# Moving the router's turn and product behind the last chunks of the output projection in an encoder layer

## The chip, the cores and the metric

The kernel runs on one core of a Trainium2 chip. The time is that of the device in microseconds (us), the median over the runs shown. The engines are TensorE (PE, its weight loads apart as PEld), VectorE (DVE), ScalarE (ACT), GpSimd (POOL), and SyncE (SP), which issues nearly all transfers.

## The reference

One layer of an encoder: a token mixer (attention over latents beside a short convolution), cross attention to 256 memory tokens, and a mixture of 32 experts, each followed by a residual and a layer norm. The tokens are 1024 of a prompt and 8 groups of 16 samples, each with memory keys and values of its own. The part that matters here is the second step, and the router's logits behind it:

```python
def cross_attend(x, mk, mv, w_xq, w_xo):
    q = (x @ w_xq).reshape(B, S, X_HEADS, X_HEAD_DIM)
    sc = jnp.einsum('bqhd,bmhd->bhqm', q, mk).astype(jnp.float32) * X_SCALE
    p = jax.nn.softmax(sc, axis=-1).astype(mv.dtype)
    o = jnp.einsum('bhqm,bmhd->bqhd', p, mv).reshape(B, S, D_MODEL)
    return o @ w_xo
...
x = layer_norm(ALPHA * x + a, lp['ln1_g'], lp['ln1_b'])
x = layer_norm(ALPHA * x + cross_attend(x, mk, mv, lp['w_xq'], lp['w_xo']), lp['ln2_g'], lp['ln2_b'])
x = layer_norm(ALPHA * x + hier_moe(x, lp), lp['ln3_g'], lp['ln3_b'])
...
logits_g = (xt @ lp['w_router_group']).astype(jnp.float32) + lp['b_router_group'].astype(jnp.float32)
logits_e = (xt @ lp['w_router_expert']).astype(jnp.float32).reshape(T, N_GROUPS, EXPERTS_PER_GROUP)
```

D_MODEL is 1024, the four memory heads are 256 wide, and the router has 4 + 32 = 36 columns.

## The kernel before

Every engine has its own program, written out by hand, and they meet in counting semaphores. The tokens are nine tiles of 128 rows: tiles 0 to 7 the prompt, tile 8 the samples. The change lies in one stage: the output projection of the cross attention (w_xo), tile by tile, and woven into it the cross attention of the eight sample groups, one group to one prompt tile.

**TensorE.** `outward(t, ks)` multiplies tile t by chunks ks of w_xo, eight chunks in all, in three products of high and low halves (`three_products`, L911, six matmuls of 512 columns to a chunk). It writes the PSUM tile M[t % 2]. Between the pairs of chunks stand the steps of sample group t and of what is left of group t-1:

- `weigh_memory_rows(t-1)` (L1063) weighs the values, `turn_memory_rows(t-1)` turns the result (two transposes).
- `turn_memory(t, 0)` and `turn_memory(t, 1)` turn the keys of group t (eight transposes each, to T[0]); ScalarE copies the first half out (L1494), VectorE the second (L1913).
- `memory_scores(t)` (L1048) computes the scores, sixteen matmul records over four strips of 32 columns. `turn_weights(t)` turns the softmax weights (two transposes).
- `turn_x2(t-1)` turns the normed rows of tile t-1 (eight transposes to T[0]), ScalarE copies them to x2T (L1483), and `route_rows(t-1)` (L1101) multiplies them by the router: eight matmuls, sixteen records, of 36 columns into M[(t-1) % 2].

All transposes are recorded at L689. Since tile t+1 uses the same PSUM tile as the logits of t-1, `outward` opens with

```python
                        else:
                            pe.wait_ge(logits_done, 2 + t - 1)
```

**VectorE**, for each tile: the sample's query rows (L1911), the second half of the turned keys (L1913), the scores' maximum (L1915), the reciprocal of the sum (L1917); `add_logits(t-1)` (L1851), which adds the router's bias and frees the PSUM tile; then, when projection t is done (product_ps), `add_rows` (L1754 to L1760: residual sum, statistics) and `norm_rows` (L1764, L1767). Between these two, GpSimd works out the inverse deviation (L2118, L2120). GpSimd also splits the rows of a later tile (`out_low`, L2173), of the last tile too.

**ScalarE**, for each tile: the high half of the rows of tile t+1 (L1467), the weighed rows of group t-1 (L1472), the first half of the turned keys (L1494), the turned rows of group t-1 (L1476), `turn_x2(t-1)`, that is the copy to x2T (L1483), exp of the scores (L1499), the turned weights (L1502).

**SyncE**, for each tile: values of group t (L604), keys of group t+1 (L601), the store of normed tile t-1 (L598), and the load of the residual rows of tile t+1 (L594), which waits for turn_x2(t-1), because it overwrites what that step reads. The first half of expert 0's weights (L625) is queued behind the last of these.

Behind the eight prompt tiles TensorE runs weigh_memory_rows(7), turn_x2(7), turn_memory_rows(7), route_rows(7) and the whole of projection 8; then come the router's ranks (L1132 to L1153) and the expert stage.

Of the kernel before, what the change touches and what calls it, by code (L numbers as in the profile page):

```python
# [49 lines left out]
def encoder_layer_kernel(nc, A, O):  # L50
# [4 lines left out]
    P, D, NT, PT = 128, 1024, 9, 8  # L55
# [54 lines left out]
    with ctx:  # L110
# [572 lines left out]
        def _(pe):  # L683
# [3 lines left out]
            def transposes(out, rows, n, width=P):  # L687
                for k in range(n):
                    got = nc.tensor.transpose(out[:, k * P:(k + 1) * P] if width == P else out[0:width, k * P:(k + 1) * P],  # L689
                                              rows[:, k * width:(k + 1) * width], ident)  # L690
                return got
# [214 lines left out]
            def three_products(out, hi, lo, k):  # L906

                for x, parts in ((hi, (high, low)), (lo, (high,))):
                    for c in (0, 512):
                        for part in parts:  # L910
                            got = nc.tensor.matmul(out[:, c:c + 512], x[k], part(k)[:, c:c + 512],  # L911
                                                   start=(k == 0 and x is hi and part is high), stop=(k == KT - 1 and x is lo))
                return got

            def chunks(rows):
                return [rows[:, k * P:(k + 1) * P] for k in range(KT)]
# [125 lines left out]
            def memory_scores(b):  # L1042
                pe.wait_ge(mkT_lo, b + 1)
                pe.wait_ge(mkT_hi, b + 1)
                pe.wait_ge(sxq_ready, b + 1)
                for h in range(XH):
                    for c in (0, 1):
                        got = nc.tensor.matmul(T[1][h * 32:(h + 1) * 32, 0:MEM], qx_b[:, 2 * h + c, :], mkT_b[:, 2 * h + c, :],  # L1048
                                               start=(c == 0), stop=(c == 1))
                got.then_inc(sb_ps, 1)  # L1050

            def turn_weights(b):
                pe.wait_ge(sb_exp, NB + b + 1)
                transposes(T[1][:, 256:512], px_b, 2).then_inc(pTb_ps, 1)
# [18 lines left out]
            def outward(t, ks):  # L1073
                u = t % 2
                for k in ks:
                    if k == 0:
                        pe.wait_ge(rows_high, 2 * NT + t + 1)
                        pe.wait_ge(o_low, t + 1)
                        if t < 2:
                            pe.wait_ge((oT_first, oT_second)[u], 4)  # L1080
                        else:
                            pe.wait_ge(logits_done, 2 + t - 1)
                    if t == 0:
                        pe.wait_ge(w_low, 3 * KT + k + 1)
                    got = three_products(M[u], chunks(rows_hi[u]), chunks(rows_lo[u]), k)
                    if t == PT:
                        got.then_inc(w_used, 1)
                if k == KT - 1 and t < PT:
                    got.then_inc(product_ps, 1)
# [15 lines left out]
            for t in range(PT):  # L1105
                outward(t, (0, 1))
                if t > 0:
                    weigh_memory_rows(t - 1)
                if t > 1:
                    pe.wait_ge(x2T_ready, t - 1)  # L1110
                turn_memory(t, 0)
                outward(t, (2, 3))
                if t > 0:
                    turn_memory_rows(t - 1)
                turn_memory(t, 1)
                outward(t, (4, 5))
                if t > 0:
                    turn_x2(t - 1)
                memory_scores(t)
                if t > 0:  # L1120
                    route_rows(t - 1)
                outward(t, (6, 7))
                turn_weights(t)
            weigh_memory_rows(NB - 1)
            turn_x2(PT - 1)
            turn_memory_rows(NB - 1)
# [131 lines left out]
        def _(act):  # L1258
# [220 lines left out]
            def turn_x2(t):  # L1479
                act.wait_ge(rowsT_ps, 2 * NT + t + 1)  # L1480
                if t > 0:
                    act.wait_ge(router_ps, t)
                nc.scalar.copy(x2T.rearrange("p k c -> p (k c)"), T[0][:, :]).then_inc(x2T_ready, 1)  # L1483

            out_high(0)
            for t in range(PT):
                if t < PT - 1:
                    out_high(t + 1)
                if t > 0:
                    memory_rows(t - 1)  # L1490
                act.wait_ge(mkT_ps, 2 * t + 1)
                if t > 0:
                    act.wait_ge(sb_ps, NB + t)
                nc.scalar.copy(mkT_b[:, :, 0:P], T[0][:, :].rearrange("p (k c) -> p k c", k=KT)).then_inc(mkT_lo, 1)  # L1494
                if t > 0:
                    memory_rows_turned(t - 1)
                    turn_x2(t - 1)
                act.wait_ge(sb_negmax, NB + t + 1)
                nc.scalar.activation(px_b, T[1][:, 0:MEM], ACT.Exp, bias=negmax[0][:, 0:1], scale=1.0,  # L1499
                                     accum_out=rsum[0][:, 0:1]).then_inc(sb_exp, 1)  # L1500
                act.wait_ge(pTb_ps, NB + t + 1)
                nc.scalar.copy(pxT_b.rearrange("p c q -> p (c q)"), T[1][:, 256:512]).then_inc(pTb_ready, 1)  # L1502
            memory_rows(NB - 1)
# [115 lines left out]
        def _(dve):  # L1619
# [133 lines left out]
            def add_rows(n, u, x, r):  # L1753
                nc.vector.scalar_tensor_tensor(r[u], x[u], ALPHA, M[u][:, :], ALU.mult, ALU.add).then_inc(sum_done, 1)  # L1754
                dve.wait_ge(sum_done, n + 1)
                nc.vector.bn_stats(stats[u][:, 0:6], r[u][:, 0:512])
                nc.vector.bn_stats(stats[u][:, 6:12], r[u][:, 512:]).then_inc(dve_step, step.next())
                dve.wait_ge(dve_step, step.value())
                dve.sem_inc(waited, 1)
                nc.vector.bn_aggr(moments[u][:, :], stats[u][:, :]).then_inc(var_ready, 1)  # L1760

            def norm_rows(n, u, x, r, gain, shift):
                dve.wait_ge(var_ready, n + 1)
                nc.vector.scalar_tensor_tensor(r[u], r[u], moments[u][:, 0:1], gain, ALU.subtract, ALU.mult).then_inc(dve_step, step.next())  # L1764
                dve.wait_ge(dve_step, step.value())
                dve.wait_ge(rstd_ready, n + 1)
                return nc.vector.scalar_tensor_tensor(x[u], r[u], rstd[u][:, 0:1], shift, ALU.mult, ALU.add)  # L1767
# [81 lines left out]
            def add_logits(t):  # L1849
                dve.wait_ge(router_ps, t + 1)  # L1850
                nc.vector.tensor_tensor(logits[:, t, :], M[t % 2][:, 0:NG + NE], b_router[:, :], ALU.add).then_inc(logits_done, 1)  # L1851
# [53 lines left out]
            for t in range(NT):  # L1905
                u = t % 2
                if t < PT:
                    b = t
                    if b > 0:
                        dve.wait_ge(sb_ps, NB + b)  # L1910
                    nc.vector.tensor_copy(qx_b[:, :, 0:ROWS], qxT_s[:, :, b * ROWS:(b + 1) * ROWS]).then_inc(sxq_ready, 1)  # L1911
                    dve.wait_ge(mkT_ps, 2 * b + 2)
                    nc.vector.tensor_copy(mkT_b[:, :, P:], T[0][:, :].rearrange("p (k c) -> p k c", k=KT)).then_inc(mkT_hi, 1)  # L1913
                    dve.wait_ge(sb_ps, NB + b + 1)
                    nc.vector.tensor_reduce(negmax[0][:, 0:1], T[1][:, 0:MEM], AX.X, ALU.max, negate=True).then_inc(sb_negmax, 1)  # L1915
                    dve.wait_ge(sb_exp, NB + b + 1)
                    nc.vector.reciprocal(rinv[b % 2][:, 0:1], rsum[0][:, 0:1]).then_inc(sb_p, 1)  # L1917
                    if t > 0:
                        add_logits(t - 1)
                    dve.wait_ge(product_ps, PT + t + 1)  # L1920
                else:
                    add_logits(PT - 1)
                    pick_experts(slice(0, PT), PT)
                    split_gate_up(0, range(5))
                    dve.wait_ge(w_used, 3 * KT)
                dve.wait_ge(x_in[u], 16 * (3 * (5 - u) + t // 2))
                add_rows(NT + t, u, xr2, res2)
                norm_rows(NT + t, u, xr2, res2, gain2, shift2).then_inc(norm_ready, 1)
            slots = slot_id.rearrange("p t k -> p k t")

# [345 lines left out]
```

## Time and profile before

| | |
|---|---|
| median of 3 runs | 1724.16 us (1723.03 to 1727.54) |
| the profiled execution | 1727.54 us, its span 1725.5 us |
| TensorE busy | 1606.8 us, 93% of the span |
| TensorE's weight loads | 1291.3 us, 75% |
| VectorE busy | 993.1 us, 58% |
| ScalarE busy | 752.6 us, 44% |
| GpSimd busy | 256.9 us, 15% |
| mean granted clock | 0.976 |

The span is the time from the first to the last instruction of the profiled execution. Busy shares are means over stages that differ. The chain that ended last is followed back from the last instruction: at each step to what released it. Its pieces are cut where the next begins, while the timeline gives each instruction's full duration; so the same matmuls appear a little longer there. The granted clock is TensorE's: 1.00 is 2.4 GHz, 0.50 is 1.2 GHz.

### The profile page before, as it was taken

The page shows a single profiled execution, that of the slowest core. Times are in us where ns is not written, and L with a number is a line of the kernel's source. Part 1 is how long each engine was busy: PE and PEld are TensorE (multiplying, and loading weights), DVE is VectorE, ACT ScalarE, POOL GpSimd, SP SyncE. Part 2 cuts the span into 40 slices and gives each one's busy share as a digit, 9 for nine tenths or more (in the row PEclk, how much of TensorE's full clock was granted, in tenths as well). Part 3 has the DMA queues.
Part 4 walks back from the last instruction along what each step waited for, and adds up shares of the span by engine and source line. Part 5 has one row for each costly group of instructions (what it writes and reads, how often), then busy time and mean ns, then how long its engine had stood idle before and what let it go on. Part 6 is the DMA issues. An engine that isn't in the chain of part 4 may idle for free.

```text
span 1725.5 us, 21728 instructions
## 1 busy us (share of the span) xinstructions
PE 1606.8 (93%) x8282; PEld 1291.3 (75%) x8282; DVE 993.1 (58%) x1347; ACT 752.6 (44%) x1062; POOL 256.9 (15%) x210
## 2 busy tenths in 40 slices
PE   8999999799998899999999989899999999999966
PEld 4578877467766688899877867788888888888842
DVE  1410111366765365422255447888889898898936
ACT  2311111322334301322242213678878777888834
POOL 0000000000006174000011121121111111111104
PEclk9999999999999999999999996999999999999988
DMA  9510111600002354400045554799999999999967
GB/s 353 214 63 33 65 53 47 241 20 17 13 12 98 131 170 176 171 25 13 1 162 180 172 171 171 284 383 385 372 385 378 380 389 383 395 380 376 362 237 295
DMA packets 134295, 351.77 MB, mean 204 GB/s; under 512 B 24498, under 2 KB 27186, under 8 KB 128708
## 3 DMA queue, kind: packets, MB, share of 16 engines
q1 hardware_dynamic: 124084, 330.69, 52.0%
q0 software_dynamic: 9216, 18.89, 2.9%
q10 hardware_dynamic: 912, 1.05, 0.3%
q8 instruction: 56, 0.92, 0.2%
q14 instruction: 27, 0.22, 0.0%
HBM read 322.19 MB, written 43.15 MB: 212 GB/s over the span
## 4 chain that ended last, share of the span: by engine, by line
PE 61%; DMA 18%; DVE 13%; ACT 4%; issue 3%; SPq 1%; POOL 0%; DVEq 0%; POOLq 0%; ACTq 0%
DMA beside<-in_w_exp_up 16%; PE M L911 12%; DVE rounded L1628 10%; PE T L753 6%; PE M L744 5%; PE M L1159 5%; PE T L689 4%; PE M L816 3%; PE T L806 3%; PE M L689 2%; PE T L970 2%; PE T L972 2%; PE T L971 2%; ACT rounded L1516 2%; PE M L999 2%
## 5 line engine op out<-in xcount | busy, mean ns | idle before, releaser
L1159 PE MATMUL M<-rounded 128*128 128x512 f32 x2304 | 547.9, 395 | 11.1 <-DVE conv_w_rows L1959 5.6
L1628 DVE TENSOR_TENSOR rounded<-beside,rounded 128x1024 fp32r<-128x1024 f32 (+2 forms) x394 | 467.8, 1234 | 113.8 <-ACT rounded L1516 56.6
L1159 PEld LDWEIGHTS M<-rounded 128*128 128x128 f32 x2304 | 429.4, 189 | 104.3 <-issue 13.7
L1516 ACT CAST rounded<-beside 128x1024 fp32r<-128x1024 f32 x256 | 259.2, 1049 | 95.5 <-DMA beside<-in_w_exp_up 88.4
L911 PE MATMUL M<-rounded 128*128 128x512 f32 x864 | 209.6, 397 | 3.0 <-ACT rounded L1388 1.6
L911 PEld LDWEIGHTS M<-rounded 128*128 128x128 f32 x864 | 160.4, 190 | 36.2 <-issue 2.2
L1526 ACT CAST rounded<-beside 128x1024 fp32r<-128x1024 f32 x128 | 125.3, 1048 | 18.3 <-DMA beside<-in_w_exp_down 15.9
L2200 POOL DMA_INDIRECT expert_rows<-beside,route_out x32 | 45.1, 1410 | 375.0 <-ACT beside L1557 355.1
L689 PE MATMUL T<-tables,arena 128*128 128x128 f32 x572 | 80.4, 287 | 19.0 <-DMA arena<-in_mem_prompt 7.1
L1341 ACT ACTIVATE arena<-T,negmax 128x384 f32<-128x384 f32 (+3 forms) x64 | 47.4, 741 | 114.5 <-DVE negmax L1705 114.5
L689 PEld LDWEIGHTS T<-tables,arena 128*128 128x128 f32 x572 | 70.2, 148 | 36.3 <-issue 12.7
L1628 DVE TENSOR_TENSOR rounded<-T,rounded 128x512 fp32r<-128x512 f32 (+1 forms) x82 | 81.7, 1000 | 26.7 <-ACT rounded L1401 18.2
L806 PE MATMUL T<-arena 96*128 96x384 f32 (+3 forms) x192 | 71.8, 489 | 10.8 <-issue 10.8
L816 PEld LDWEIGHTS M<-arena 128*128 128x128 f32 x576 | 71.8, 191 | 10.3 <-issue 7.7
L744 PE MATMUL M<-rounded,x_high 128*128 128x416 f32 (+1 forms) x270 | 70.4, 374 | 6.6 <-DVE x_low L1628 6.6
L970 PE MATMUL T<-rounded 128*128 128x256 f32 x256 | 73.1, 285 | 2.4 <-issue 2.4
L816 PE MATMUL M<-arena 128*128 x576 | 72.5, 271 | 0.7
L971 PE MATMUL T<-rounded 128*128 128x256 f32 x256 | 72.4, 283 | 0.0
L972 PE MATMUL T<-rounded 128*128 128x256 f32 x256 | 72.4, 283 | 0.0
L2193 POOL DMA_INDIRECT beside<-x_rows,route_tok x32 | 50.4, 1575 | 142.0 <-PE T L1200 121.0
L753 PE MATMUL T<-rounded,x_high 128*128 128x512 f32 x270 | 65.3, 394 | 0.0
L753 PEld LDWEIGHTS T<-rounded,x_high 128*128 128x128 f32 x270 | 50.7, 188 | 11.7
(302 smaller groups left out, 2121.3 us busy)
## 6 DMA issues: line engine op xcount, KB each, us to landing
beside<-in_w_exp_gate SPq DMA_DIRECT2D x64, 1024.0 KB, 7.9
beside<-in_w_exp_up SPq DMA_DIRECT2D x64, 1024.0 KB, 11.1
beside<-in_w_exp_down SPq DMA_DIRECT2D x32, 2048.0 KB, 11.4
arena<-x_rows SPq DMA_DIRECT2D x27, 512.0 KB, 4.6
x_rows<-arena SPq DMA_DIRECT2D x18, 512.0 KB, 3.2
arena<-expert_rows SPq DMA_DIRECT2D x9, 1024.0 KB, 12.9
arena<-in_x_prompt SPq DMA_DIRECT2D x16, 512.0 KB, 4.1
arena<-in_cache_mem_k SPq DMA_DIRECT2D x8, 1024.0 KB, 5.7
```

Source lines behind the costliest of these rows:

```text
L689: got = nc.tensor.transpose(out[:, k * P:(k + 1) * P] if width == P else out[0:width, k * P:(k + 1) * P], rows[:, k * width:(k + 1) * widt ...
L744: got = nc.tensor.matmul(M[u][:, at:at + c1 - c0], x[:, k * P:(k + 1) * P], part[k][:, c0:c1], start=(k == 0 and part is w_in_high and x i ...
L753: got = nc.tensor.matmul(T[u][:, c:c + CW], x[:, k * P:(k + 1) * P], part[k][:, GC + c:GC + c + CW], start=(k == 0 and part is w_in_high a ...
L806: got = nc.tensor.matmul(T[n % 2][:, c:c1], qT[u][0:HW, i * P:(i + 1) * P], kT[u][0:HW, c:c1], start=True, stop=True)
L816: got = nc.tensor.matmul(o, prT[n % 2][:, c, :], value[:, c, ds(h * DV, DV)], start=(c == 0), stop=(c == i))
L911: got = nc.tensor.matmul(out[:, c:c + 512], x[k], part(k)[:, c:c + 512], start=(k == 0 and x is hi and part is high), stop=(k == KT - 1 an ...
L970: nc.tensor.matmul(out, high(k)[:, d * P:(d + 1) * P], x1T[:, 0, k], start=(k == 0), stop=False)
L971: nc.tensor.matmul(out, high(k)[:, d * P:(d + 1) * P], x1T[:, 1, k], start=False, stop=False)
L1159: got = nc.tensor.matmul(out, x[xs], (high, low)[ws](w)[:, c:c + 512], start=(first and n == 0), stop=(last and n == 2))
L1516: nc.scalar.copy(high(c), w_raw[c // 4][:, c % 4, :]).then_inc(gu_high, 1)
L1526: nc.scalar.copy(high(8 + c), w_raw[2][:, c, :]).then_inc(down_high, 1)
L1628: return nc.vector.tensor_tensor(out, x, highs.bitcast(f32), ALU.subtract)
```

## The change

On TensorE, `turn_x2(t-1)` and `route_rows(t-1)` move behind chunks 6 and 7 of projection t, with `turn_weights(t)` between them; `memory_scores(t)` comes ahead of those chunks by itself. ScalarE's copy to x2T moves behind exp. VectorE's `add_logits(t-1)` moves behind `add_rows(t)`, ahead of `norm_rows(t)`. No instruction is added or taken away.

```diff
@@ TensorE, for each tile t
                 outward(t, (4, 5))
+                memory_scores(t)
+                outward(t, (6, 7))
                 if t > 0:
                     turn_x2(t - 1)
-                memory_scores(t)
+                turn_weights(t)
                 if t > 0:
                     route_rows(t - 1)
-                outward(t, (6, 7))
-                turn_weights(t)
@@ ScalarE, for each tile t
                 if t > 0:
                     memory_rows_turned(t - 1)
-                    turn_x2(t - 1)
                 act.wait_ge(sb_negmax, NB + t + 1)
                 nc.scalar.activation(px_b, T[1][:, 0:MEM], ACT.Exp, bias=negmax[0][:, 0:1], scale=1.0,
                                      accum_out=rsum[0][:, 0:1]).then_inc(sb_exp, 1)
+                if t > 0:
+                    turn_x2(t - 1)
                 act.wait_ge(pTb_ps, NB + t + 1)
@@ VectorE, for each tile t
                     nc.vector.reciprocal(rinv[b % 2][:, 0:1], rsum[0][:, 0:1]).then_inc(sb_p, 1)
-                    if t > 0:
-                        add_logits(t - 1)
                     dve.wait_ge(product_ps, PT + t + 1)
...
                 dve.wait_ge(x_in[u], 16 * (3 * (5 - u) + t // 2))
                 add_rows(NT + t, u, xr2, res2)
+                if 0 < t < PT:
+                    add_logits(t - 1)
                 norm_rows(NT + t, u, xr2, res2, gain2, shift2).then_inc(norm_ready, 1)
```

## Rows read from the trace of the kernel before

**Rows 1.** Chain that ended last, one interval (start us, us, engine, tile, line, count).

```profile
953.60 0.22 PE T L689 x2
953.82 2.75 PE M L911 x12
...
965.21 0.89 PE T L689 x8
966.10 0.02 issue
966.12 1.02 ACT arena L1483
967.14 0.04 issue
967.19 1.98 PE M L1101 x16
969.16 2.85 PE M L911 x12
972.01 0.22 PE T L689 x2
```

**Rows 2.** Timeline of the same interval (start us, us, instruction, idle before it, releaser).

```profile
966.02 1.09 PE L1048 MATMUL T<-arena 128*32 128x256 f32 x16
...
969.20 0.20 DVE L1851 TENSOR_TENSOR logits<-M,b_router 128x36 f32<-128x36 f32 x1 [0.78 <-PE M L1101]
970.42 0.34 SPq L594 DMA_DIRECT2D arena<-x_rows  x1
...
972.05 1.22 DVE L1754 SCALAR_TENSOR_TENSOR arena<-arena,M 128x1024 f32<-128x1024 f32 x1 [2.65 <-PE M L911]
...
974.99 1.28 DVE L1764 SCALAR_TENSOR_TENSOR arena<-arena,moments 128x1024 f32<-128x1024 f32 x1
...
976.96 2.41 POOL L2173 TENSOR_TENSOR rounded<-beside,rounded 128x1024 fp32r<-128x1024 f32 x1
...
977.11 3.34 DVE L1767 SCALAR_TENSOR_TENSOR arena<-arena,rstd,shift 128x1024 f32<-128x1024 f32 x1 [0.84 <-POOL rstd L2120]
...
980.91 1.23 DVE L1913 COPY arena<-T 128x1024 f32<-128x1024 f32 x1 [0.32 <-PE T L689]
```

**Rows 3.** Chain that ended last, projection 0.

```profile
894.35 1.02 PE T L1048 x16
895.37 2.99 PE M L911 x12
```

**Rows 4.** End of the stage: chain that ended last, then one row of the timeline.

```profile
1032.35 1.29 DVE arena L1767
1033.69 1.98 PE T L689 x8
...
1036.76 3.63 PE M L1101 x16
...
1040.46 13.01 PE M L911 x48
...
1038.02 2.34 POOL L2173 TENSOR_TENSOR rounded<-beside,rounded 128x1024 fp32r<-128x1024 f32 x1 [5.79 <-ACT rounded L1467]
```

**Rows 5.** Windows by stretch: busy us (records) by engine, granted clock, DMA share, GB/s.

```profile
546.00:549.40 3.40, 3.40 (x11) 2.15 (x10) 1.21 (x2) 0.40 (x1) 3.32 (x3) 0.51 0.00 0
...
1008.80:1027.20 18.40, 18.32 (x126) 14.56 (x125) 7.78 (x11) 3.71 (x7) 3.56 (x4) 1.00 0.59 210
1029.02:1030.70 1.68, 0.01 (x1) 0.00 (x0) 1.49 (x4) 0.47 (x1) 0.31 (x1) 1.00 0.24 88
1030.70:1040.40 9.70, 6.03 (x26) 5.49 (x26) 2.10 (x2) 2.23 (x3) 3.79 (x3) 0.50 0.00 0
...
1055.70:1058.00 2.30, 2.30 (x23) 2.30 (x22) 1.85 (x3) 0.00 (x0) 1.31 (x2) 1.00 0.00 0
1058.00:1060.20 2.20, 2.20 (x13) 2.20 (x13) 1.61 (x3) 0.00 (x0) 0.46 (x1) 0.51 0.00 0
```

## The prediction

> **What bounds the kernel now.** I first read the page's busy shares and the slices of the span: TensorE is the fullest engine, and in the stage of the change (its last matmuls end at 1053 us, [rows 4]) nothing else is close. Then I read the chain that ended last through one interval of that stage, from the end of one projection's last chunk to the end of the next; I call the end of chunks 6 and 7 of projection t P(t), and it is the place just ahead of the two transposes of turn_weights. [rows 1] show an interval of 18.41 us (953.60 to 972.01) in which TensorE is on the chain all the time but for one step: ScalarE's copy x2T (L1483), with 0.06 us of hand-over around it. So every microsecond of order lost on TensorE is lost for the kernel. The timeline of the same interval [rows 2] shows what is hidden: the sixteen matmuls of memory_scores (L1048, 1.09 us) run under that copy, and VectorE does its work with time to spare. The windows by stretch [rows 5] give the granted clock: 1.00 in the eighth interval, which stands for all eight, so the stage runs at 2.4 GHz.
>
> **What the change does, step by step.** Three orders change: TensorE's, ScalarE's, VectorE's. No instruction is added or removed, and no DMA is.
>
> TensorE. Before, turn_x2(t-1) stands ahead of memory_scores(t), and route_rows(t-1) behind it, both ahead of chunks 6 and 7. After, both steps stand behind chunks 6 and 7, and between them only turn_weights(t), two transposes.
>
> *First interval.* P(0) to P(1) no longer holds turn_x2(0), the copy, and route_rows(0): 0.89, 1.08 (966.10 to 967.19) and 1.97 us [rows 1]. The scores, so far under the copy, come onto the chain with 1.02 us, as they stand in the chain of projection 0, which has no such copy [rows 3]. 1.02 - 0.89 - 1.08 - 1.97 = -2.92 us.
>
> *The next six intervals*, P(1) to P(7), hold the same steps again, one interval late. Three things differ. The scores are no longer under the copy: +1.02. The two transposes of turn_weights are: -0.22 [rows 1]. And a wait comes up that was never felt: outward(t+1) starts with a wait for the logits of rows t-1, since it overwrites their PSUM tile. Before, add_logits came 0.04 us behind the last route matmul (969.16 to 969.20) and TensorE had chunks 6 and 7 to do meanwhile [rows 1, 2]; now route_rows is the last thing ahead of that wait: 0.04 for VectorE to start, 0.20 for L1851, 0.05 for TensorE to start again (the copy's hand-over is 0.04 to 0.05), 0.29 us. The first weight load behind such a wait is not hidden under a matmul. The trace has no such restart of this matmul; it can cost from nothing to one load of a 128x128 block, 0.2 us at the most (a pair of load and matmul takes 2.75 / 12 = 0.23). I take the middle, 0.1. Per interval 1.02 - 0.22 + 0.29 + 0.1 = 1.19 us, six times: +7.1 (6.5 to 7.7).
>
> VectorE. add_logits(t-1) now stands behind the sums and statistics of add_rows(t), which are done at P + 2.98 (972.01 to 974.99), and ahead of norm_rows(t). The route matmuls end at P + 0.89 + 1.08 + 1.97 = P + 3.94, so VectorE waits for about 1 us, and L1764 starts at P + 4.2 instead of P + 2.98. Queued behind it: L1764, L1767, and then the two copies that the next scores need. In the six intervals this is covered. L1764 could now meet GpSimd's subtraction L2173 (2.41 us from P + 4.95), which stretches L1767 to 3.34 us where it takes 1.29 alone [rows 2, 4]; at the worst the norm is done at P + 9.3 instead of P + 8.44, and the copy L1913 isn't wanted before TensorE has done the ten transposes, at P + 8.9 before and at P + 12.9 now. Without that cover it would cost up to 0.9 us an interval. *At the end of the stage* there is no cover: TensorE waits for norm_rows(7). There L1764 ends at P + 4.2 + 1.28, and L1767 can start at P + 5.55 where it started at P + 5.10: +0.45 us.
>
> ScalarE's two swapped steps cost nothing: exp now finds its scores earlier, the copy x2T waits for TensorE, and the next reader of its queue (pxT_b) has until the next interval. SyncE's queue is touched by one wait: load_x1(t+1) asks for turn_x2(t-1), so it moves from P - 1.6 (970.42) to about P + 0.9; its data are for P(t+1), over 17 us later. The first expert's load is queued behind the last of them, and moves from a place of no need to another.
>
> Sum of the order: -2.9 + 7.1 + 0.45 = +4.6 us (4.0 to 5.2).
>
> **The clock.** What the order leaves behind each P(1) to P(7) is a thin stretch: from P + 0.89 to P + 4.2, 3.3 us, TensorE does two transposes and sixteen matmuls of 36 columns, and stands still for 0.9 and 0.3 us. Before, such matmuls had scores ahead of them and full 512-column matmuls behind, and the clock stayed. The trace shows what thin stretches do: it fell to 0.50 (1.2 GHz) after 1.7 us of standing still behind projection 7, and again at 1058.0 after 2.3 us in which TensorE's record is 2.30 of 2.30 us busy, but with 32-column matmuls (L1138) [rows 5]. The new stretch is thinner than the second and longer than both. I take it that the clock falls in five of the six intervals; not in all, because the route steps of before never made it fall, and so a full matmul close by seems able to save it. Price: the shortest fall within the work shown lasts from 546.0 to 549.4 at 0.51 [rows 5]. 3.4 us at half speed lose 1.7 us where TensorE is full, less where part of them meets waits; I take 1.4. Five times: +7.0, between 0 and 6 x 1.7 = 10.2. The end of the stage is at half clock before (1030.7 on: turn_x2 1.98 for 0.89, route 3.63 for 1.98) [rows 4, 5] and stays so. If the fall comes already during route_rows(6), the logits are up to 1.65 later; 0 taken.
>
> The Trainium skill, "TensorE: Matmul & The Clock Gate", section "HAM oscillation — how this bites in real kernels", ties the fall to gaps in which TensorE waits between bursts. By that rule the waits of 0.9 and 0.3 us would be harmless, and the sum would be the order's alone, +4.6 us. The fall at 1058.0, with no wait ahead of it, does not fit that rule taken alone.
>
> **Sum.** 4.6 + 7.0 = +11.6 us. The profiled execution would go from a span of 1725.5 to 1737.1 and from 1727.54 to 1739.1 us of its own. It is the slowest of the three runs shown, 3.4 us over their median, so against the median: 1724.16 + 11.6 = 1735.8 us.
>
> **Rivals.**
> *The clock holds.* Order costs only: 1728.8 us. For it: it stayed at 1.00 through eight intervals with the same route matmuls. Against it: the fall at 1058.0, and that each of six thin stretches would have to pass. 0.23.
> *It ends faster.* The fall behind projection 7 goes away: turn_x2(6) and route_rows(6) now fill part of TensorE's idle time there, and if that holds the clock, turn_x2(7) gains 1.1, route_rows(7) 1.65 and the first part of outward(8) about 2.0 (13.01 us for 48 matmuls where 4 x 2.75 would be 11.0) [rows 1, 4]. GpSimd's row split for projection 8 (L2173) ends together with route_rows(7) today, at 1040.36 and 1040.39 [rows 4], and outward(8) waits for both, so the 1.65 is given back: 3.1 us net. It decides only if the six intervals cost less than 0.05 us each: -2.9 + 0.45 - 3.1 = -5.6, 1718.6 us. Against it: the copy of 1.02 us stands in each of them with 0.22 under it. 0.04.
> *More than counted.* VectorE's late norm holds the copy for the next scores, or route_rows at half clock makes both later: 0.9 more for each of six, +17 us, 1741 us. Against it: 3.6 us of cover. 0.09.
> *The forecast*, three or more falls: 0.64, by itself 1732 to 1740.
>
> **How the numbers follow.** The likeliest case gives 1735.8. The range reaches down to the clock that holds, 1728.0, and up to 1740.5, the order's sum with falls in all six at their full price (4.6 + 10.2 + 1.65). 0.3% of this kernel is 5.2 us, about what a measurement can tell from no change; above 1729.3 counts as slower. All of the forecast and of the dearer case are there, and a small part of the clock that holds (4.6 is just under 5.2): 0.64 + 0.09 + 0.03 = 0.76. The rest of it is the same: 0.20. Faster: 0.04.
>
> **What the profile after would show.** P(0) to P(1) 15.5 us instead of 18.4. The later intervals 19.6 us without a fall and about 21 with one. Behind each P(1) to P(6) on the chain: eight transposes, L1483, L1101, then L1851, which the chain of before has not, and then L911. L1048 on the chain in every projection. L1764 1.2 us later behind P. Granted clock under 1 in five of six intervals; if it is 1.00 in all, my largest term is wrong. If P(1) comes 2.9 us sooner but the later intervals stay at 18.4, the wait for the logits or the bare copy was misjudged. If the expert stage is longer or shorter by more than 1 us, something moved that I hold to be only shifted.

## The result, and the profile after

The changed kernel takes 1740.38 us (median of 6 runs, 1736.91 to 1742.66), and the kernel before 1725.85 us beside it (6 runs, 1723.03 to 1732.11). The ratio is 1.0082, with a 95% interval from 1.0057 to 1.0105: slower, by 14.2 us (9.8 to 18.1; the two medians alone are 14.5 apart). The profiled execution took 1737.2 us, with a span of 1735.4 us.

The chain that ended last, of the changed kernel: P(0) and P(1), and then the interval from P(2) to P(3) (start us, us, engine, tile, line, count). The interval of before is in [rows 1].

```profile
894.53 0.22 PE T L689 x2
...
906.14 1.02 PE T L1048 x16
907.16 2.99 PE M L911 x12
910.15 0.89 PE T L689 x8
...
931.55 0.89 PE T L689 x8
932.47 1.02 ACT arena L1483
...
933.53 1.99 PE M L1101 x16
935.52 0.02 issue
935.54 0.20 DVE logits L1852
935.75 0.14 issue
935.88 3.00 PE M L911 x12
...
948.54 2.99 PE M L911 x12
951.53 0.89 PE T L689 x8
```

P(0) to P(1) went from 18.41 to 15.62 us (894.53 to 910.15). A later interval took 19.98 us (931.55 to 951.53). In it stand, one behind another, what the prediction put there: eight transposes, the copy, the route matmuls, and VectorE's L1852, which is add_logits and was L1851 before. It was on no chain of this stage then. The scores (L1048) are on the chain, since no copy hides them.

But that interval is the cheaper kind. Windows by stretch, from each P to the next (busy us and records of PE, PEld, DVE, ACT and POOL, then the granted clock, DMA share and GB/s):

```profile
894.50:910.10 15.60, 15.60 (x102) 11.84 (x101) 9.25 (x10) 3.64 (x7) 4.13 (x3) 1.00 0.51 168
910.10:931.50 21.40, 20.14 (x126) 15.70 (x125) 9.37 (x11) 4.55 (x8) 3.11 (x3) 0.92 0.46 148
931.50:951.50 20.00, 18.74 (x127) 14.64 (x126) 9.41 (x11) 4.55 (x8) 3.14 (x3) 1.00 0.50 159
951.50:974.40 22.90, 21.64 (x127) 16.59 (x126) 9.06 (x11) 4.55 (x8) 3.10 (x3) 0.85 0.42 138
974.40:995.90 21.50, 20.23 (x126) 15.71 (x125) 9.38 (x11) 4.55 (x8) 3.12 (x3) 0.92 0.45 147
995.90:1015.90 20.00, 18.74 (x127) 14.66 (x126) 9.39 (x11) 4.55 (x8) 3.12 (x3) 1.00 0.49 158
1015.90:1037.30 21.40, 20.14 (x127) 15.68 (x125) 7.33 (x11) 3.60 (x7) 2.58 (x4) 0.92 0.32 100
```

In four of the six later intervals TensorE's clock fell. In the profile of before it was 1.00 in all seven, of which [rows 5] shows one. Each fall came at the end of the thin stretch: the block of L911 behind it took 4.39, 5.46, 4.57 and 4.42 us in those four intervals, and 3.00 and 2.97 us in the other two. One fall costs 1.4 to 1.6 us (21.4 and 21.56 against 19.97), and the one that lasted twice as long 2.9 us (22.86). From P(0) to P(7) the changed kernel takes 142.77 us (894.53 to 1037.30), the one before 7 x 18.41 = 128.87: 13.9 us more. Of these 15.62 + 6 x 19.97 - 128.87 = 6.6 are the order's, and 7.3 the clock's.

What follows is nearly as it was. The chain behind P(7), to be held against [rows 4]:

```profile
1041.28 0.07 DVE logits L1852
...
1041.39 1.29 DVE arena L1765
...
1042.71 1.30 DVE arena L1768
...
1044.05 1.98 PE T L689 x8
...
1047.12 3.65 PE M L1101 x16
```

turn_x2(7) begins 6.75 us behind P(7), 6.42 before (1033.69 - 1027.27): 0.3 us later, and again at half clock. The span grew by 9.9 us only, because P(0) came 3.8 us sooner in this execution: the profile of before has three stretches at half clock more, or longer ones, ahead of the stage, the one in [rows 5] at 546.0 among them. That differs from one execution to the next; the 14.2 us come from the runs.

### The profile page after: what moved, and what is told of

It reads as the page before. It is cut to its first block, busy times and chain, and to the rows that moved or that the text cites. A ratio compares the mean times of both kernels' runs of the same rounds, so it can differ in the third digit from the quotient of the medians.

```text
span 1735.4 us, 21728 instructions
## 1 busy us (share of the span) xinstructions
PE 1612.0 (93%) x8282; PEld 1292.7 (74%) x8282; DVE 993.6 (57%) x1347; ACT 751.8 (43%) x1062; POOL 249.4 (14%) x210
## 4 chain that ended last, share of the span: by engine, by line
PE 58%; DMA 20%; DVE 13%; ACT 4%; issue 3%; SPq 1%; POOL 0%; DVEq 0%; POOLq 0%; ACTq 0%
DMA beside<-in_w_exp_up 18%; PE M L911 11%; DVE rounded L1629 10%; PE T L753 6%; PE M L744 5%; PE M L816 3%; PE T L689 3%; PE M L1159 3%; PE T L806 3%; PE M L689 2%; PE T L970 2%; ACT rounded L1517 2%; PE T L972 2%; PE T L971 2%; PE M L999 2%
## 5 line engine op out<-in xcount | busy, mean ns | idle before, releaser
L1159 PE MATMUL M<-rounded 128*128 128x512 f32 x2304 | 548.9, 395 | 11.2 <-DVE conv_w_rows L1960 5.6
L911 PE MATMUL M<-rounded 128*128 128x512 f32 x864 | 216.5, 407 | 5.2 <-DVE logits L1852 2.3
L911 PEld LDWEIGHTS M<-rounded 128*128 128x128 f32 x864 | 164.9, 195 | 43.6 <-issue 7.9
L1527 ACT CAST rounded<-beside 128x1024 fp32r<-128x1024 f32 x128 | 125.3, 1048 | 19.5 <-DMA beside<-in_w_exp_down 17.2
L816 PEld LDWEIGHTS M<-arena 128*128 128x128 f32 x576 | 71.8, 192 | 10.3 <-issue 7.7
## 6 DMA issues: line engine op xcount, KB each, us to landing
beside<-in_w_exp_down SPq DMA_DIRECT2D x32, 2048.0 KB, 11.6
```

What stands on the lines that cost most here:

```text
L816: got = nc.tensor.matmul(o, prT[n % 2][:, c, :], value[:, c, ds(h * DV, DV)], start=(c == 0), stop=(c == i))
L1159: got = nc.tensor.matmul(out, x[xs], (high, low)[ws](w)[:, c:c + 512], start=(first and n == 0), stop=(last and n == 2))
L1527: nc.scalar.copy(high(8 + c), w_raw[2][:, c, :]).then_inc(down_high, 1)
```

## The experiments

Each ran beside the kernel before, and the ratios are to it; only ratios compare runs of different groups. The median of before was 1724.77 us for one group (the one wide matmul, the three narrow ones, turn_x2 moved back, and TensorE's and ScalarE's edits alone), 1726.08 for VectorE's edit alone and projection 7 alone, 1726.44 for the changed kernel again, the five wide matmuls, the logits apart and the clock held behind P(7), and 1725.16 for the four wide matmuls alone and the four chunks. Each kernel has one profile, so a count of falls is that of one execution.

**The changed kernel again** (no edit).

> The changed kernel once more, beside the kernels of this group. Theory: where the falls come is chance, as the intervals meet the clock's own count at another point in each execution; the order is not. So P(0) to P(1) is 15.62 us again and an interval without a fall 19.95 to 20.0, with one 21.3 to 21.6, but the number of falls in the six is between two and five; ratio to before 1.007 to 1.009. Rival, that the falls are at fixed intervals: again in the second, fourth, fifth and seventh.

Measured: 1739.69 us, ratio 1.0081 (1.0064 to 1.0098). Windows by stretch: a fall, placed within its interval (P(1) is at 909.17), and the two dearest intervals:

```profile
909.00:913.00 4.00, 3.12 (x27) 2.86 (x25) 2.72 (x4) 2.23 (x3) 0.60 (x2) 1.00 0.24 61
913.00:916.40 3.40, 3.02 (x9) 2.35 (x9) 3.24 (x2) 0.00 (x0) 2.51 (x2) 0.52 0.22 88
...
950.50:973.40 22.90, 21.64 (x127) 16.52 (x125) 9.15 (x12) 4.55 (x8) 3.10 (x3) 0.85 0.43 138
...
994.90:1017.80 22.90, 21.64 (x127) 16.53 (x125) 9.10 (x11) 4.55 (x8) 3.10 (x3) 0.85 0.43 138
```

The clock fell 3.8 us behind P(1), at the end of the thin stretch. The order repeats: P(0) to P(1) is 15.6 us again, and 19.94 in the one interval of six that kept its clock. The falls do not: five intervals had one, two of them of the long kind, and the falls cost 10.3 us of 145.8. So the number of falls varies from one execution to another, and with it the time.

**One wide matmul in the wait for the copy.**

```diff
                 turn_weights(t)
+                if t > 0:
+                    nc.tensor.matmul(M[(t - 1) % 2][:, 512:1024], ident, tables[:, 0:512], start=True, stop=True)
                 if t > 0:
                     route_rows(t - 1)
```

> The changed kernel, and in each of the seven intervals one more matmul of full width (a 128x128 block by 512 columns of fp32, result never read) behind turn_weights, in the time in which TensorE waits for the copy to x2T (0.88 us in the profile after). It takes about 0.85 us at 2.4 GHz, so it lengthens nothing by itself. Theory that the thin stretch behind P brings the clock down (falls cost 7.4 of 13.9 us in the stage of the profile after): with the stretch filled the falls in the intervals go, from four to one or none; the stage from P(0) to P(7) takes about 135.5 us, not 142.8, and the kernel is 5 to 7 us faster than the changed one, some 1733 us, ratio to before 1.004. Rival that the falls come from elsewhere, or that what matters is the wait for the logits: four to five falls stay, the stage stays at 142 us or longer, ratio 1.008 to 1.010.

**Three narrow ones there instead.**

```diff
                 turn_weights(t)
+                if t > 0:
+                    for n in range(3):
+                        nc.tensor.matmul(M[(t - 1) % 2][:, 512:512 + NG + NE], ident, tables[:, 0:NG + NE], start=True, stop=True)
```

> The control of the fill: the changed kernel, and in the same place three matmuls of 36 columns (six records, about 0.75 us), result never read. TensorE no longer waits there, but does not do more columns to speak of. If standing still is what brings the clock down (the rule of the Trainium skill, TensorE: Matmul & The Clock Gate, section on HAM oscillation, speaks of idle gaps alone), the falls go as with the fill, the stage takes 135 to 136 us and the ratio to before is 1.004. If short matmuls count for little, as the fall at 1058.0 in the kernel before suggested, four to six falls stay, the stage takes 141 to 146 us and the ratio is 1.008.

Measured: 1737.81 us, ratio 1.0073 (1.0059 to 1.0087) with the wide one, and 1736.86 us, 1.0069 (1.0056 to 1.0082) with the narrow ones. Both profiles have two falls in six intervals, and the others took 19.95 to 19.98 us. The falls did not go, so what I expected of the wide one was a miss, and neither run can be told from the changed kernel (1.0081, 1.0064 to 1.0098). The two falls of the wide one are those of its fastest execution (1732.69 us, 5.1 under its median), so its other executions probably had more. The control did no worse, so this pair did not tell width from standing still.

**Four wide matmuls of the fast kind in that wait, and one more behind route_rows.**

```diff
                 if t > 0:
+                    for n in range(4):
+                        nc.tensor.matmul(M[(t - 1) % 2][:, 512:1024], high(0)[:, 0:P], high(0)[:, 0:512], start=True, stop=True)
                     route_rows(t - 1)
+                    nc.tensor.matmul(M[(t - 1) % 2][:, 512:1024], high(0)[:, 0:P], high(0)[:, 0:512], start=True, stop=True)
```

> The changed kernel with more in the thin stretch than the first fill had: four 512-column matmuls of the fast kind (0.21 us each) in the wait for the copy and one more behind route_rows, in the wait for the logits; results never read. All in time in which TensorE stood still. Theory: the first fill went only part of the way (two falls in six intervals, and so had the control with short matmuls, in one profile each); with five wide matmuls the falls in the intervals go, none or one of six, all intervals 19.95 to 20.1 us, stage 135.5 us, ratio to before 1.004 (1732 to 1733 us), 5 us or more faster than the changed kernel beside it. Rival, that filling does not hold the clock: two to four falls, ratio 1.006 to 1.008.

Measured: 1731.87 us, ratio 1.0029 (1.0015 to 1.0042), against 1.0081 (1.0064 to 1.0098) for the changed kernel in the same group. The wait and the thin stretch in its chain, and the window of that interval; the other five read the same, at 1.00:

```profile
951.14 1.09 PE T L689 x10
952.23 0.93 PE M L1124 x4
953.16 1.94 PE M L1101 x16
955.09 0.31 PE M L1126
955.40 0.07 issue
955.47 3.00 PE M L911 x12
```

```profile
951.20:971.20 20.00, 19.93 (x132) 15.38 (x131) 9.42 (x12) 4.55 (x8) 3.14 (x3) 1.00 0.50 158
```

TensorE did five matmuls more in each interval, the interval stayed at 19.96 to 19.99 us, and the clock did not fall once. The stage took 135.44 us. That is the order's cost by itself (6.6 us), and the kernel is 7.8 us faster than the changed one beside it: the price of the falls, shown by taking them away. A small part lies behind the stage, since projection 7 got the filling too: from its sum to that of projection 8 it was 25.99 us, and 26.40 in the changed kernel's profile.

**The four alone, without the one behind route_rows.**

```diff
                 if t > 0:
+                    for n in range(4):
+                        nc.tensor.matmul(M[(t - 1) % 2][:, 512:1024], high(0)[:, 0:P], high(0)[:, 0:512], start=True, stop=True)
                     route_rows(t - 1)
```

> The changed kernel with the four wide fast matmuls in the wait for the copy, but none behind route_rows. Theory: TensorE's time in the gap is then as full as with the five, and the 0.2 us behind route_rows matter little by themselves; none to two falls in the six intervals, stage 135.5 to 138.5 us, ratio to before 1.003 to 1.006. Rival, that the count behind route_rows is what tips it (the first fill filled the same gap, with the slow kind of matmul, and had two falls): two falls or more, ratio 1.006 to 1.008, as with the first fill.

Measured: 1735.70 us, ratio 1.0055 (1.0039 to 1.0071), two falls in six intervals (21.55 and 21.56 us). The fifth matmul, 0.3 us in the wait for the logits, seems to hold the last of them. The more of the stretch is filled with wide work, the fewer falls: none filled, four and five; the first wait, two; both, none. The ratios follow, at 1.0081, 1.0055 and 1.0029. The intervals of neighbours touch (1.0064 to 1.0098, 1.0039 to 1.0071, 1.0015 to 1.0042), so only the two ends are told apart for certain, and what the fifth matmul does by itself is suggested, not shown.

**The logits of tiles 0 to 6 in a bank of their own.**

```diff
+        def logits_at(t):
+            return M[t % 2][:, 0:NG + NE] if t > PT - 2 else T[1][:, 512:512 + NG + NE]
...
@@ weigh_memory_rows(b)
+                pe.wait_ge(logits_done, 2 + b)
@@ outward(t, ks)
-                            pe.wait_ge(logits_done, 2 + t - 1)
+                            pe.wait_ge(sum_done, NT + t - 1)
```

> The changed kernel with the logits of tiles 0 to 6 in a bank of their own (free columns of T[1]), so that projection t+1 no longer waits for add_logits(t-1), only for add_rows(t-1), long done. Theory: the wait behind route_rows (0.02 + 0.20 + 0.14 us in the profile after) goes from each of six intervals, and L911's first block starts at once: 19.6 us without a fall instead of 19.97, 2.1 us in all, and fewer or as many falls; ratio 1.005 to 1.008. Rival, that this wait is the larger part of the loss, as the copy would be hidden otherwise: intervals of 18.9 us or less.

Measured: 1738.28 us, ratio 1.0069 (1.0050 to 1.0088). Windows of an interval with a fall and of one without:

```profile
931.70:952.70 21.00, 20.12 (x127) 15.65 (x125) 9.39 (x11) 4.55 (x8) 3.12 (x3) 0.92 0.48 151
952.70:972.20 19.50, 18.62 (x127) 14.60 (x126) 9.42 (x11) 4.55 (x8) 3.15 (x3) 1.00 0.48 162
```

An interval without a fall is 19.45 us, 0.52 less: the wait for the logits (0.36) and the restart behind it (the first block of L911 took 2.85 us instead of 3.00). Four of six had a fall all the same, so the fall does not need that wait. It is a small term, as predicted, and not the larger part of the loss.

**turn_x2(t-1) back ahead of chunks 6 and 7, route_rows(t-1) behind them.**

```diff
                 memory_scores(t)
-                outward(t, (6, 7))
                 if t > 0:
                     turn_x2(t - 1)
+                outward(t, (6, 7))
                 turn_weights(t)
```

> The changed kernel with turn_x2(t-1) back ahead of chunks 6 and 7 (behind the scores), route_rows(t-1) left behind them. The copy runs under those chunks. Theory: an interval loses the wait of 0.9 us: about 18.9 us without a fall, for 19.96; P(0) to P(1) is 16.5 us. The stretch behind P is shorter (2.5 us, not 3.4), so fewer falls: none to three. The order costs about +1.5 us against before, with falls up to +6: ratio 1.001 to 1.003. Rival that the route matmuls and the logits at the end of the interval are the cost and not the copy: intervals stay above 19.5 us, four falls or more, ratio 1.007.

Measured: 1737.39 us, ratio 1.0074 (1.0057 to 1.0091). The intervals without a fall took 19.57 and 19.59 us, and four of six had one. The theory's 18.9 us was wrong, the rival (19.5 us or more, four falls, 1.007) came true, and the chain says why:

```profile
977.51 0.02 issue
977.53 1.23 DVE arena L1755
...
978.78 0.69 DVE stats L1757
...
980.43 0.07 DVE logits L1852
980.50 0.14 issue
980.64 2.98 PE M L911 x12
```

The copy is hidden and route_rows done early, but add_logits stands behind the residual sum and the statistics, which end 2.9 us behind P. TensorE waits for VectorE until P + 3.1. In the changed kernel both waits lie side by side: take one away, and the other holds the interval at 0.4 us less.

**VectorE's edit alone**, all else as before.

```diff
-                    if t > 0:
-                        add_logits(t - 1)
                     dve.wait_ge(product_ps, PT + t + 1)
...
                 add_rows(NT + t, u, xr2, res2)
+                if 0 < t < PT:
+                    add_logits(t - 1)
```

> The kernel before with the change on VectorE alone: add_logits(t-1) behind add_rows(t); TensorE and ScalarE as before. Theory: the wait for the logits at the head of outward(t+1) is then the bound: TensorE has only turn_weights ahead of it, and the logits are there at P + 2.98 + 0.2, so each of seven intervals is about 3.0 us longer (21.4 instead of 18.41), 21 us in all, and as TensorE stands still for 3 us the clock falls in most intervals, for another 5 to 10 us: 1752 us, ratio 1.013 to 1.019. Rival, that this wait is covered: ratio 1.000.

Measured: 1752.75 us, ratio 1.0155 (1.0140 to 1.0169). The first interval stayed at 18.41 us, as it has no logits to wait for, and the six later ones took 21.6 us, or 23.1 to 23.2 with a fall (three of them). So it was six times 3.2 us, not seven times 3.0. It also bears on the falls: here TensorE stood still for 2.9 us behind each P, with two transposes ahead of that wait and the route matmuls back in their old place, and the clock fell in three of six intervals. A wait alone can bring a fall too.

```profile
914.50:936.10 21.60, 18.59 (x127) 14.60 (x124) 9.31 (x11) 4.65 (x8) 4.12 (x3) 1.00 0.45 146
936.10:959.30 23.20, 20.19 (x127) 15.66 (x124) 9.30 (x11) 4.66 (x8) 4.10 (x3) 0.93 0.45 141
```

**TensorE's and ScalarE's edits alone**; against the changed kernel:

```diff
+                    if t > 0:
+                        add_logits(t - 1)
                     dve.wait_ge(product_ps, PT + t + 1)
...
                 add_rows(NT + t, u, xr2, res2)
-                if 0 < t < PT:
-                    add_logits(t - 1)
```

> The changed kernel with VectorE's order as before: add_logits(t-1) ahead of the wait for projection t. Theory: TensorE's intervals stay as in the changed kernel (15.6, then 20.0, 21.4 with a fall), as route_rows ends later than the statistics anyway; but add_rows(7) now starts behind the logits, 4.2 us after P(7) instead of at once, and nothing covers it: the tail is 3.7 us longer, ratio to before 1.010 (1743 us). Rival, that VectorE's new place is a cause of the loss: ratio 1.004 or less.

Measured: 1744.98 us, ratio 1.0113 (1.0095 to 1.0131, four runs), against 1.0073, 1.0069 and 1.0074 for the others of its group and 1.0082 (1.0057 to 1.0105) for the changed kernel, whose interval meets it. The profile shows the difference: L1755, the sum, starts at 1045.54 behind the last route matmul instead of at P(7) (1041.13), and turn_x2(7) 10.79 us behind P(7) instead of 6.75, 4.0 us later where 3.7 were expected. VectorE's new place is a help given TensorE's order, and a cost of its own without it.

**The change for projection 7 alone**; against the kernel before, ScalarE's and VectorE's edits under the same two conditions:

```diff
                 outward(t, (4, 5))
-                if t > 0:
+                if 0 < t < PT - 1:
                     turn_x2(t - 1)
                 memory_scores(t)
-                if t > 0:
+                if 0 < t < PT - 1:
                     route_rows(t - 1)
                 outward(t, (6, 7))
+                if t == PT - 1:
+                    turn_x2(t - 1)
                 turn_weights(t)
+                if t == PT - 1:
+                    route_rows(t - 1)
```

> The kernel before, and the change for projection 7 alone, on all three engines: only there do turn_x2(6), route_rows(6), the copy and add_logits(6) stand behind chunks 6 and 7, where TensorE waits for the norm anyway. Theory: P(7) comes 2.9 us sooner (P(6) to P(7) 15.5 us instead of 18.41), the six intervals ahead of it stay at 18.41 without a fall, and the norm behind it is 0.3 us later: 2.6 us faster than before, ratio 0.9985, between 0.997 and 1.000. Rival, that what the first interval gained in the changed kernel is lost again behind P(7), as route_rows(6) delays the norm or keeps TensorE from the steps behind it: ratio 1.000 or more.

Measured: 1723.36 us, ratio 0.9989 (0.9976 to 1.0002). In its profile the six intervals ahead took 18.40 to 18.41 us, and P(6) to P(7) 15.62. The last interval's two ends in the chain, each the first step behind chunks 6 and 7:

```profile
1008.94 0.22 PE T L689 x2
...
1024.56 0.89 PE T L689 x8
```

The gain is there in the trace (126.05 us from P(0) to P(7), for 128.89), and in the runs at the edge of what they tell: the interval reaches over 1.

**The same, with the clock held behind P(7)** by wide matmuls wherever TensorE would stand still.

```diff
+            def keep_busy(count):
+                for n in range(count):
+                    nc.tensor.matmul(M[0][:, 512:1024], high(0)[:, 0:P], high(0)[:, 0:512], start=True, stop=True)
...
                 if t == PT - 1:
+                    keep_busy(4)
                     route_rows(t - 1)
+                    keep_busy(1)
             weigh_memory_rows(NB - 1)
+            keep_busy(7)
             turn_x2(PT - 1)
             turn_memory_rows(NB - 1)
+            keep_busy(3)
             route_rows(PT - 1)
+            keep_busy(7)
             outward(PT, range(KT))
```

> The kernel with the change for projection 7 alone, and behind P(7) wide matmuls whose result is never read wherever TensorE would stand still: four ahead of route_rows(6), one behind it, seven ahead of turn_x2(7), three under its copy, seven behind route_rows(7). Theory: the clock does not fall behind P(7) (0.50 from 1030.7 to 1044.4 in the profile before): turn_x2(7) takes 0.9 us instead of 1.98, route_rows(7) 2.0 instead of 3.63, outward(8) 11 us instead of 13.01; the row split on GpSimd gives back 1.65. Another 3.1 us: ratio to before 0.997, 5.6 us faster, projection 7's sum to projection 8's sum 23 us instead of 26.2. Rival, that what follows was not waiting for TensorE (VectorE's experts' split is on the chain there in the profile after): ratio 0.9985 to 1.000 although the clock holds.

Measured: 1722.91 us, ratio 0.9984 (0.9967 to 1.0000). Windows by stretch behind P(7):

```profile
1024.20:1030.90 6.70, 6.70 (x54) 5.14 (x52) 5.39 (x7) 1.76 (x3) 0.78 (x2) 1.00 0.72 255
...
1037.00:1048.00 11.00, 11.00 (x49) 9.10 (x50) 10.42 (x27) 5.01 (x7) 0.00 (x0) 1.00 0.72 241
```

The clock held, and outward(8) took 11 us instead of 13.01 [rows 4]. Yet from projection 7's sum to projection 8's it was 25.25 us, not 23 (26.39 without the filling). The chain of that stretch:

```profile
1037.37 9.82 DMA beside<-in_w_exp_up
...
1047.22 1.06 ACT rounded L1532
...
1048.34 1.11 issue
1049.45 1.23 DVE arena L1770
```

The sum (L1770) waits in VectorE's queue behind the split of expert 0's fifth chunk, whose weights landed at 1047.2. The rival of this run was right: what follows was not waiting for TensorE alone.

**The same, with four chunks ahead of the sum instead of five.**

```diff
-                    split_gate_up(0, range(5))
+                    split_gate_up(0, range(4))
...
-            split_gate_up(0, range(5, KT))
+            split_gate_up(0, range(4, KT))
```

> The kernel with the change for projection 7 alone and the clock held behind P(7), and on VectorE four instead of five chunks of expert 0's split ahead of add_rows(8); the fifth goes behind, to the other three. In the profile of the held clock outward(8) was done at 1048.1 us, but VectorE's sum came at 1049.45, behind the fifth chunk's split, which waits for the transfer of w_exp_up (landed at 1047.2). Theory: the sum comes at 1048.2, 1.2 us sooner, from projection 7's sum to projection 8's 24.0 us instead of 25.25, and the kernel is 1.2 us faster than with the held clock: ratio to before 0.9975 to 0.998. Rival, that the gather of the first rows and expert 0's eight chunks then wait for VectorE: no gain, ratio 0.9985.

Measured: 1722.48 us, ratio 0.9980 (0.9968 to 0.9991), the only version whose interval lies wholly under 1: faster than the kernel before by 3.4 us (1.6 to 5.5; the medians are 2.7 apart). From sum to sum it took 23.97 us, as expected. Against the version ahead of it the runs can't tell a gain; the profile shows 1.3 us.

## Why the prediction was right

It said 1735.8 us, 11.6 more than before; measured were 1740.38 us, 14.2 more. The way and the mechanism came out: an order that costs, and on top of it a clock that falls behind the thin stretch. The size fitted with some luck. The range ended at 1740.5 (its parts, 4.6 + 10.2 + 1.65 on 1724.16, add up to 1740.6), so the median lies 0.1 us inside, and it got that far up because the range allowed for six falls at full price, and for 1.65 us of late logits that did not come (route_rows(6) took 1.99 us). The order by itself was put at 4.0 to 5.2 us and was 6.9, outside. By its steps:

**The first interval**: 2.9 us less were predicted, and 2.79 measured. The chunks behind the scores take 2.99 us, not the 2.85 that they took behind route_rows.

**The six intervals**: +1.19 us each was predicted, and 1.56 measured (19.97), 9.4 us instead of 7.1. The scores (+1.02) and turn_weights (-0.22) came as worked out. The term that was mis-sized is the wait for the logits with its restart: 0.02 + 0.20 + 0.14 and a first block of 3.00 instead of 2.75 us make 0.61, where I had 0.39. The wake-up of TensorE was 0.14 and not 0.05. Of the block's 0.25, the run with the logits apart leaves 0.10 without any wait (2.85), as that block took behind route_rows in [rows 1]; the restart is the other 0.15, within the 0 to 0.2 that I had allowed. The chunks behind the scores are the other 0.14.

**The norm**: +0.45 us behind P(7) was predicted, 0.33 measured: L1765 starts at P + 4.09 and not P + 4.2, as it follows 0.11 us behind the start of L1852 and does not wait for its 0.20. In the six intervals L1764, now L1765, did meet GpSimd's row split, as feared, and was covered, as said:

```profile
934.69 0.22 POOL L2119 TENSOR_SCALAR moments<-moments 128x1 f32<-128x1 f32 x1 [18.21 <-DVE moments L1761]
...
935.52 2.40 POOL L2174 TENSOR_TENSOR rounded<-beside,rounded 128x1024 fp32r<-128x1024 f32 x1
...
935.66 3.34 DVE L1765 SCALAR_TENSOR_TENSOR arena<-arena,moments 128x1024 f32<-128x1024 f32 x1
...
939.03 1.28 DVE L1768 SCALAR_TENSOR_TENSOR arena<-arena,rstd,shift 128x1024 f32<-128x1024 f32 x1
...
944.81 1.23 DVE L1914 COPY arena<-T 128x1024 f32<-128x1024 f32 x1 [4.36 <-PE T L689]
```

The norm is done 8.8 us behind P (931.55), and the copy waits another 4.36 us for TensorE.

**The clock**: five falls at 1.4, 7.0 us, were predicted. Four in one profile cost 7.3 us, five in the other 10.3, and taking them away gained 7.8. A fall costs 1.4 to 1.6, or 2.9 when the stretch at half clock is twice as long, which I had not counted. So the clock's total came out right over two things that were not: fewer falls in that profile than the five assumed, and one dearer than any assumed. The rival that the clock holds had the order alone at 4.6 us; with the clock held by added work the median is 5.4 us over the one of before beside it (1731.87 for 1726.44), a ratio of 1.0029, just within the 0.3% that I had called no change.

**The cause of the falls.** The prediction set the rule of the Trainium skill ("TensorE: Matmul & The Clock Gate", section "HAM oscillation — how this bites in real kernels"), which names gaps in which TensorE waits, against the fall at 1058.0. The runs bear out the thin stretch as the place: the falls came at its end, and filled with wide work in both waits it made none in the profile taken. With the first wait filled by narrow matmuls, TensorE stood still there for 0.3 us instead of 0.9 and two falls stayed; with the wait for the logits taken away four stayed. With one long wait and no route matmuls beside it (VectorE's edit alone) there were three. So no single one of the two waits is the cause, and waiting plays a part. Whether it is all of it stays open: the narrow filling had as few falls as the wide one of the same length, each in one profile, and no run here isolates how much narrow matmuls count.

**The rival on the other side**, that the fall behind P(7) goes away: it did not in the changed kernel. Its price was put at 3.1 us, and it is 1.1 with the change for projection 7 alone (26.39 to 25.25 us from sum to sum). VectorE's queue took 1.3 of the rest, as the version with four chunks ahead of the sum shows; for the other 0.7 no run has a cause.

## What to carry to other kernels

A step that is moved from under one wait to behind a full block brings its own waits into the open. Here ScalarE's copy of the turned rows had let the scores run for nothing under it, and VectorE's read that frees the PSUM tile was free because chunks 6 and 7 stood behind it; the new order gave up both. In the traces the same move is worth 2.8 us, less 0.3 for the norm, where the engine idles anyway (behind the last projection), and costs 1.6 us where it doesn't, so apply it to that one turn of the loop. And in this stage, which TensorE bounds, a row of short waits and narrow matmuls cost twice: once for its time, and once for the clock that fell behind it.

## What the runs showed that I had not expected

GpSimd's add on a 128x1 column (L2118 before, L2119 after) took 1.20 us in each interval before, where it started beside VectorE's L1764 (two SBUF inputs). After, VectorE stood still at that time, and it took 0.22 us (934.69, shown above). Behind P(7) that gained nothing: L1765 started at 1041.39 only, when the deviation had just been done (1041.29), and even a step of 1.20 us would have been done before L1765 ended. The Trainium skill, "GPSIMD Engine Reference", section "1. Specifications", says that GpSimd shares its SBUF interfaces with VectorE, with contention from VectorE's instructions of two SBUF inputs; the trace agrees, with 1.20 against 0.22 us, and 3.34 against 1.28 us the other way, for VectorE's L1765 beside L2174.

A wide filling of 0.85 us in time in which TensorE only waited was free: the intervals were 19.95 to 19.99 us with it and without it, and with five matmuls of the fast kind in the two waits the kernel gained 7.8 us.
